# A gated activation folded into one ScalarE step, rows added by halves, and a last norm on two engines, in a two-block transformer kernel

## The reference, cut to what matters

```
def expert_block(args):
    xb, e = args
    gu = xb @ w1[e] + b1[e]
    gate, up = jnp.split(gu, 2, axis=-1)
    gate = jnp.minimum(gate, SWIGLU_LIMIT)          # 7.0
    up = jnp.clip(up, -SWIGLU_LIMIT, SWIGLU_LIMIT)
    glu = gate * jax.nn.sigmoid(SWIGLU_ALPHA * gate)  # 1.702
    return ((up + 1.0) * glu) @ w2[e] + b2[e]
...
x = x + g2[:, None, :] * _moe(h, w_router[l], b_router[l], w1[l], b1[l], w2[l], b2[l])
...
return _rmsnorm(x, final_g)
```

## Time and profile before

| | us |
|---|---|
| runs shown, median (lowest to highest) | 1909.75 (1908.7 to 1909.96) |
| the profiled execution, its own time | 1911.13 |
| its span in the trace | 1909.1 |
| busy PE / DVE / ACT / POOL | 1616.4 / 470.0 / 249.8 / 116.0 |
| second mixture, first w1 matmul to last row added | 961.7 to 1900.0 |

### The profile page before, as it was taken

The page is one execution under the profiler, slowest core; times in us unless marked ns, Lnnn a source line. Parts: engine busy times, 40 slices in busy tenths (PEclk is TensorE's granted clock), DMA queues, the critical chain, the costliest instruction groups (busy, mean ns, idle before and its releaser), DMA issues. The chain is left out here.

```text
span 1909.1 us, 23699 instructions
## 1 busy us (share of the span) xinstructions
PE 1616.4 (85%) x9872; PEld 783.0 (41%) x9872; DVE 470.0 (25%) x749; ACT 249.8 (13%) x451; POOL 116.0 (6%) x267
## 2 busy tenths in 40 slices
PE   6999998676766667797799898989989989899896
PEld 6665545333323334464543333333333333333332
DVE  2632313110101100597421121221221212212123
ACT  2123322000000001114210000000000000000001
POOL 0030000793000000000000000000000000000000
PEclk9999998888778888897799999999999999999998
DMA  9556875999999999613568999999999999999994
GB/s 327 211 177 252 270 264 200 426 426 428 428 428 428 428 428 424 220 76 146 229 290 355 428 428 426 428 427 428 428 428 428 427 428 427 427 427 428 428 428 196
DMA packets 90270, 683.75 MB, mean 358 GB/s; under 512 B 18103, under 2 KB 21352, under 8 KB 53352
## 3 DMA queue, kind: packets, MB, share of 16 engines
q1 hardware_dynamic: 86466, 678.72, 86.3%
q10 hardware_dynamic: 3750, 4.26, 0.7%
HBM read 681.91 MB, written 1.05 MB: 358 GB/s over the span
## 5 line engine op out<-in xcount | busy, mean ns | idle before, releaser
L1391 PE MATMUL ps<-ring,hT 128*64 128x512 f32 x2048 | 464.4, 611 | 38.9 <-DMA ring<-in_w_dram 38.8
L1391 PEld LDWEIGHTS ps<-ring,hT 128*64 128x64 f32 x2048 | 158.1, 141 | 342.3 <-issue 341.4
L1386 PE MATMUL ps<-ring,hT 128*32 128x256 f32 x2048 | 161.6, 481 | 95.5 <-DMA ring<-in_w_up_dram 60.9
L1434 PE MATMUL ps<-ring,Wp 128*64 128x512 f32 x992 | 224.7, 612 | 14.3 <-ACT Wp L1476 14.3
L1386 PEld LDWEIGHTS ps<-ring,hT 128*32 128x32 f32 x2048 | 81.8, 133 | 176.4 <-issue 122.8
L1434 PEld LDWEIGHTS ps<-ring,Wp 128*64 128x64 f32 x992 | 71.7, 141 | 157.6 <-issue 139.7
L1525 DVE TENSOR_SCALAR Wp<-ps 128x1024 f32<-128x1024 f32 x16 | 19.6, 1225 | 430.0 <-PE ps L1391 430.0
L967 PE MATMUL ps<-ring,hT 128*128 128x512 f32 (+1 forms) x288 | 120.8, 573 | 0.0
L1469 ACT ACTIVATE mod<-Wp 128x1024 f32<-128x1024 f32 x16 | 17.0, 1061 | 782.5 <-DVE Wp L1525 782.5
L1430 PE MATMUL ps<-ring,m_hidT 128*32 128x512 f32 x480 | 69.2, 729 | 31.5 <-DMA ring<-in_w_down_dram 31.5
L1541 DVE TENSOR_TENSOR hT<-ps,Wp 128x512 f32<-128x512 f32 x32 | 20.6, 686 | 240.3 <-PE ps L1434 240.3
(11 more groups left out here) (453 smaller groups left out, 1435.2 us busy)
## 6 DMA issues: line engine op xcount, KB each, us to landing
ring<-in_w_dram SPq DMA_DIRECT2D x190, 2048.0 KB, 15.6
ring<-in_w_gate_dram SPq DMA_DIRECT2D x32, 2048.0 KB, 19.0
ring<-in_w_up_dram SPq DMA_DIRECT2D x32, 2048.0 KB, 20.1
ring<-in_w_down_dram SPq DMA_DIRECT2D x30, 2048.0 KB, 20.2
ring<-in_w_in_dram SPq DMA_DIRECT2D x14, 2048.0 KB, 15.6
ring<-in_w_ada_dram SPq DMA_DIRECT2D x12, 2048.0 KB, 11.4
ring<-in_w_out_dram SPq DMA_DIRECT2D x4, 2048.0 KB, 16.7
Wp<-in_w_down_dram SPq DMA_DIRECT2D x2, 2048.0 KB, 11.1
```

The costliest lines, as they stand in the source:

```text
L1386: ins = nt.matmul(ps[r:r + 32, u // 2, c:c + 256], xgT[:, t, x:x + 32], w[:, 512 * t:512 * t + 512].rearrange("q (p b s) -> q b p s", b=2, ...
L1391: ins = nt.matmul(ps[64 * e:64 * e + 64, b, :], xgT[:, 2 * u + t, 64 * e:64 * e + 64], w[:, c:c + 512], start=False, stop=u == 3 and t == ...
L1434: ins = nt.matmul(ps[r, C0 + h, :], hidT[:, 4 * u + t, r], w[:, c:c + 512], start=u == 0 and t == 0, stop=4 * u + t == FT - 1, tile_positi ...
```

## The change: what it does

1. The gate becomes one ScalarE step, Silu(1.702 gate) = 1.702 gate sigmoid(1.702 gate). The multiplication L1529 and its wait go away; L1532 reads `sg` and now waits for ScalarE's result and for its own engine's up half. The factor 1/1.702 goes into the copy of the transposed rows (L1476).
2. The scatter signals after each half of each tile, and VectorE adds in four steps of 512 columns, each after its own signal, in place of two of 1024.
3. In the last norm ScalarE prepares the root's table and sums the squares of tile 1 while VectorE sums those of tile 0; ScalarE's root does the scaling. Rows are multiplied in halves of 512 columns, and each half goes out by its own copy of 256 KB: tile 0's two from SyncE, tile 1's two from ScalarE's queue.

```diff
@@ pe_pair, the scatter
                             ins = nt.matmul(ps[:, (A0, C0)[i] + h, :], GT[:, i, :], y[:, 512 * h:512 * h + 512], start=True, stop=True)
-                            if h:
-                                ins.then_inc(scat, 1)
+                            ins.then_inc(scat, 1)
@@ act_pair
-                        na.activation(sg, gm, ACT.Sigmoid, scale=1.702).then_inc(act1, 1)
+                        na.activation(sg, gm, ACT.Silu, scale=1.702).then_inc(act1, 1)
...
-                        ins = na.activation(hidT[:, 4 * b:4 * b + 4, :].rearrange("p t c -> p (t c)"), ps[:, C0 + b, :], ACT.Copy)
+                        ins = na.activation(hidT[:, 4 * b:4 * b + 4, :].rearrange("p t c -> p (t c)"), ps[:, C0 + b, :], ACT.Copy,
+                                            scale=1.0 if first else 1.0 / 1.702)
@@ dve_pair
                         v.wait_ge(act1, it + 1)
-                        nv.tensor_tensor(gm, gm, sg, ALU.mult).then_inc(s("glu"), 1)
-                        v.wait_ge(s("glu"), 1)
-                        v.sem_clear(s("glu"))
+                        v.wait_ge(up_read, it + 2)
                         nv.scalar_tensor_tensor(out=hv, in0=um[:].rearrange("q (p t) -> q p t", t=FT), scalar=1.0,
-                                                in1=gm.rearrange("q (p t) -> q p t", t=FT), op0=ALU.add, op1=ALU.mult).then_inc(hid_ready, 1)
+                                                in1=sg.rearrange("q (p t) -> q p t", t=FT), op0=ALU.add, op1=ALU.mult).then_inc(hid_ready, 1)
...
+                    if not first:
+                        for h in range(2):
+                            c = slice(512 * h, 512 * h + 512)
+                            for i, (b, sm_) in enumerate(((A0, acc_a), (C0, acc_c))):
+                                v.wait_ge(scat, it * 4 + (2 * h + i + 1))
+                                ins = nv.tensor_tensor(X[:, i, c], X[:, i, c], ps[:, b + h, :], ALU.add)
+                                if h:
+                                    ins.then_inc(sm_, 1)
+                        return
@@ the last block, scalar
-                for i in range(NT):
-                    a.wait_ge(nz.sd, i + 1)
-                    nc.scalar.activation(st[:, 2 + i:3 + i], st[:, 2 + i:3 + i], ACT.Sqrt).then_inc(nz.rt, 1)
+                na = nc.scalar
+                nz.act_ready()
+                na.activation(hnf[:, 0:D], X[:, 1, :], ACT.Square, accum_out=st[:, 1:2]).then_inc(nz.sq, 1)
+                a.wait_ge(nz.sd, 1)
+                na.activation(st[:, 2:3], st[:, 0:1], ACT.Sqrt, scale=1.0 / D, bias=K("eps")).then_inc(nz.rt, 1)
+                a.wait_ge(nz.sq, 1)
+                na.activation(st[:, 3:4], st[:, 1:2], ACT.Sqrt, scale=1.0 / D, bias=K("eps")).then_inc(nz.rt, 1)
+                for h in range(2):
+                    a.wait_ge(z_x, 3 + h)
+                    a.dma_start(out[0, 128:256, HALF[h]], X[:, 1, HALF[h]]).then_inc(z_o, 16)
@@ the last block, vector
-                for i in range(NT):
-                    link(nv.tensor_tensor_reduce(out=junk[:], in0=X[:, i, :], in1=X[:, i, :], scale=1.0, scalar=0.0, op0=ALU.mult,
-                                                 op1=ALU.add, accum_out=st[:, i:i + 1]))
-                    nv.tensor_scalar(st[:, 2 + i:3 + i], st[:, i:i + 1], 1.0 / D, EPS, ALU.mult, ALU.add).then_inc(nz.sd, 1)
+                nv.tensor_tensor_reduce(out=junk[:], in0=X[:, 0, :], in1=X[:, 0, :], scale=1.0, scalar=0.0, op0=ALU.mult, op1=ALU.add,
+                                        accum_out=st[:, 0:1]).then_inc(nz.sd, 1)
                 v.wait_ge(s_grow, 64)
+                v.wait_ge(nz.sq, 1)
                 for i in range(NT):
                     v.wait_ge(nz.rt, i + 1)
                     link(nv.reciprocal(st[:, 4 + i:5 + i], st[:, 2 + i:3 + i]))
-                    nv.scalar_tensor_tensor(out=X[:, i, :], in0=X[:, i, :], scalar=st[:, 4 + i:5 + i], in1=grow[:],
-                                            op0=ALU.mult, op1=ALU.mult).then_inc(z_x, 1)
+                    for c in HALF:
+                        nv.scalar_tensor_tensor(out=X[:, i, c], in0=X[:, i, c], scalar=st[:, 4 + i:5 + i], in1=grow[:, c],
+                                                op0=ALU.mult, op1=ALU.mult).then_inc(z_x, 1)
@@ the last block, sync
-                for i in range(NT):
-                    sp.wait_ge(z_x, i + 1)
-                    sp.dma_start(out[0, i * 128:i * 128 + 128, :], X[:, i, :]).then_inc(z_o, 16)
-                sp.wait_ge(z_o, 32)
+                for h in range(2):
+                    sp.wait_ge(z_x, 1 + h)
+                    sp.dma_start(out[0, 0:128, HALF[h]], X[:, 0, HALF[h]]).then_inc(z_o, 16)
+                sp.wait_ge(z_o, 64)
```

More of the change, by code:

```diff
@@ L2386, in bass_block_pair @@
         z_x, z_o = S("normed_out"), S("out_done")
+        HALF = [slice(512 * h, 512 * h + 512) for h in range(2)]
         with nc.Block() as block:
```

## The result

The kernel after took 1901.86 us (median of seven runs, 1900.99 to 1905.47), the kernel before, measured in turns with it on the same chip, 1908.7 us (1904.76 to 1911.22). The ratio is 0.9967 with a 95% interval of 0.9956 to 0.9979: 6.3 us less, between 4.0 and 8.4. The forecast was 1907.6 with a range of 1905.5 to 1909.9 and "no change" at 0.87, so the forecast was wrong. Part of the distance is its base: the median of the three runs shown was 1909.75, that of the seven is 1908.7. The rest is a gain three times the 2.1 us forecast.

A forecast was written before the change was run, and what follows sets the result against it. Weight loads were taken to set the pace from the second mixture's third pair to the last, so only its ends count. Terms -2.0 + 0 - 0.1 = -2.1 us from 1909.75 gave 1907.6 us, range 1905.5 to 1909.9.

The forecast's parts named there:

- Part 1, first pair: Second mixture's first pair: without the VectorE step the transposes start sooner and the load stream passes it on, -1.0 us.
- Pairs 2 to 15: Middle pairs of the second mixture: the saved step is hidden under the weight loads, 0 us.
- Part 1, last pair: Last pair, after the final load wait: transposes start sooner, then limited by TensorE's bias matmuls, -1.0 us.
- Part 2: Row adds by halves at the block's end: adds finish 0.8 us sooner, hidden by TensorE's queue jump, 0 us.
- Part 3: Last norm and output: multiplications by halves +0.48 us, smaller output copy -0.6 us, together -0.1 us.
- B: VectorE's jump past the second loop grows to 3.7 us, norm 3.0 us later, 1910.6 us; chance 0.05.
- C: ScalarE stands still 1.28 us after the last norm's table load, 1908.9 us; chance 0.03.
- D: The output copy costs the same at half the size, 1908.2 us; chance 0.10.
- E: First pair's gain is lost as loads catch up, or the change misses what was named, 1908.6 to 1909.7; chance 0.06.
- F: The adds count, as VectorE and not TensorE ends the block, 1906.9 us; chance 0.05.
- Rival A: TensorE's clock in the last pair's matmul groups: neither low 1905.9 us, both low 1909.3; chances 0.13 and 0.08.
- N: Theory after the first comparison: chance in unchanged code ahead of the second mixture made the profiled pair differ.

The follow-up runs named there:

- g3: Kernel after, plus three matmuls nobody reads ahead of the first pair's transposes only; 1904.41 us, ratio 0.9987 to the kernel before.
- e2: Kernel before with only the row adds by halves, each after its own scatter signal; 1908.22 us, ratio 1.0000.
- e3: Kernel before with only the last norm on two engines and the output in four copies; 1908.0 us, ratio 0.9999.
- f1: Kernel before plus three unread matmuls ahead of the wait for the last two w1 units, from the second pair on; 1905.09 us against 1908.40, ratio 0.9982.
- f2: Kernel before plus one VectorE multiplication by 1.0 and its wait between the two products in each pair; 1909.99 us, ratio 1.0010.

## Why the prediction was wrong

From the table of traces, the means of the four traces of the kernel before and of the three of the kernel after:

| stretch | before | after | difference | forecast |
|---|---|---|---|---|
| gather to the last pair's last w1 group | 908.74 | 907.61 | -1.1 | -1.0 |
| that group's start to the w2 matmuls | 16.82 | 14.12 | -2.7 | -1.0 |
| w2 matmuls | 14.38 | 13.95 | -0.4 | 0 |
| from their end to the end of the span | 15.02 | 14.80 | -0.2 | -0.1 |
| sum from the gather on | 954.96 | 950.48 | -4.5 | -2.1 |
| ahead of the gather (not touched) | 952.15 | 949.78 | -2.4 | 0 |

**Part 1, first pair (-1.0): right.** -1.1 in the traces, and g3 shows that the path exists. **Pairs 2 to 15 (0): right**, by a period of 58.85 us and by 19.2 us more waiting for loads.

**Part 1, last pair (-1.0): right in its own step.** 1.01 of the 2.70 us is the chain's. TensorE's bias matmuls are the new limit, as forecast.

**Part 2 (0): right**, 1.0000 when measured alone, where an effect under 1.7 us would not show. The adds finish about 1 us before the norm starts, released by TensorE's queue.

**Part 3 (-0.1): right.** The first multiplication came 3.06 us after the table load (forecast 3.16), the last ended at 1895.28 + 1.41 = 1896.69, 5.99 after it (forecast 6.11), and a copy of 256 KB took 2.1 us (forecast 2.6 - 0.6 = 2.0). The estimate of 2.6 us was made with the fixed cost of about 2.0 us from the Trainium skill, "DMA: Bandwidth & Descriptors", Anatomy of one DMA. The row of 2.1 us doesn't bear that out, and that section's figures are for copies issued from GpSimd, while these come from SyncE and ScalarE. By the same figures 512 KB would take an estimated 3.2 us, where the earlier trace rows have 2.6, so the prediction's +0.5 set an estimate for the new size against a measured time for the old one. The drain that the Trainium skill, "ScalarE: Activation LUTs", What ACT_TABLE_LOAD costs, puts with a table load is not in the rows either: the next activation starts at 1892.00, right behind the load of 1.28 us that began at 1890.70. Rivals B, C and D fall with these rows. E falls with the first row of the table and with g3, F with the rows of e2.

**The step that failed** is the clock term of the last pair, put at nothing in the sum: Rival A's weight, and in it the sentence "each wait at the last units keeps its 2.7 us". The mechanism and its price were there, "1.69 us for a stretch at the lower of two levels" and "if neither is low, 1905.9", but the chance was put at 0.13 with its effect left out of the forecast. What the runs showed instead: with 1 us less in each pair the low stretch moves from the last w1 group to the third, in all three traces of the kernel after. There it is covered by the next wait, which shrinks to 1.02 us. That is 1.69 us of the gain. The trace of the kernel before could have warned of it: there too the wait ahead of a last group is not always 2.7 us, but 1.15 at 1215.96, behind a pair with both groups low. The w2 matmuls of the last pair are never low in the kernel after and were low in one of four traces of the kernel before (two of six with e2 and e3, which have the same middle stage): 0.4 us by the mean of four. Together the clock gives 2.1 us, as much as all the steps that were costed. The prediction had noted that "where the waits lie shifts by 1 us in every pair" and still took the pattern of the last pair as given.

**What stays open.** The runs give 6.3 us (4.0 to 8.4), the traces 4.5 from the gather on, which lies inside that interval, and a mean of 2.4 ahead of it, where the code is the same. By the middle values 1.8 us of the 6.3 thus have no shown cause. Over all traces with the old step (eight, f1 and f2 among them) the gather starts at 952.3 on average, over those with the new one (six) at 950.0, with spreads of 4.8 and 3.7 us. N explains a part of the 9.9 us between the two profiled executions: 954.45 - 948.96 = 5.5 of them lie there. Whether a small systematic part remains beside the chance, and through what the change could reach that stretch, is not settled. Nothing was tried that would hold that stretch fixed. Nor was it settled what decides which group runs low. The runs show only that it moves when the waits move.

## What to carry to other kernels

When some stretches of the same work run at a lower clock, look at what lies behind each: here a low stretch in front of a wait for a load was free, one in front of nothing cost its full price (1.7 us), and a small saving in a repeated stage moved it from the one place to the other. A forecast should then treat the present pattern as one outcome and not as a constant. And in a stream that is bound by loads, the pair before the stream settles and the pair after it ends are the places where a saved microsecond counts. One part alone, measured against the kernel before, is what tells the carrier of a gain from its companions.

## What was not expected of the hardware

- Added matmuls made a kernel faster: f1 takes 3.4 us less (1.7 to 5.3), with the last w1 group at 7.09 instead of 8.78 us.
- The same wait of 2.72 us stands before a group of 8.78 us and before one of 7.09 us in the same kernel, and before one of 7.09 us in the last pair of g3.
- The stretch ahead of the mixture, in code that no kernel here changes, ended between 948.5 and 954.5 us, a spread larger than the whole forecast gain.
- A step that adds 0.83 us in each pair was covered by the loads only until one pair had slow w1 and slow w2 matmuls together. Then the period went to 59.67 us.
- VectorE multiplied 1024 columns by a constant in 0.69 us (f2, L1532), two tiles of 1024 columns with each other in 1.21.
